# Mixture of experts and attention: one expert's transposes amid another's downs, weight halves with own signals, rotation ahead of values

## The chip, the cores and the metric

One Trainium2 chip, one of its cores. Time is device microseconds of one execution of the whole program; the times below are those of three runs.

## The reference

Two transformer blocks on 256 tokens of width 1024, two layers each, in float32. The second block's last layer is the one the change touches. It attends with 16 heads of 64 (8 with a forget gate, 8 with rotary positions), projects, and then runs a mixture of eight experts:

```python
def moe_swiglu(t, router, w_gate, w_up, w_down):
    logits = (t @ router).astype(jnp.float32)
    top_logits, top_idx = lax.top_k(logits, TOP_K)
    gates = jax.nn.softmax(top_logits, axis=-1)
    combine = jnp.sum(jax.nn.one_hot(top_idx, N_EXPERTS, dtype=jnp.float32) * gates[..., None], axis=1)
    out = jnp.zeros_like(t)
    for e in range(N_EXPERTS):
        out = out + combine[:, e:e + 1].astype(t.dtype) * swiglu(t, w_gate[e], w_up[e], w_down[e])
    return out
```

Each expert has gate and up weights of 1024 x 3584 and down weights of 3584 x 1024; each token goes to two of the eight.

## The kernel before

Everything is written out by hand: five engines, each with its own list of instructions, and semaphores between them. `Steps` names the signals of one engine in the order in which it gives them, so a step's place in that list has to follow the order of the instructions.

**Attention** (`pairs_tensor`, L3686) takes heads in eight pairs, the first four without rotary (fox), the last four with it (moba). For pair p PE does the scores (L3651), the next pair's queries and keys (L3597), the transposes of pair p's weights (L3666), the next pair's values (L3623), the next pair's rotation (L3634; a drain where there is no rotary) and pair p's outputs (L3681). ACT copies queries and keys (L3715), transposed weights (L3742) and values (L3720); DVE does the rope from the rotation (L3757 to L3760), on which the next scores wait.

**Experts.** The router ranks the experts by their load; rank r of the four fullest and rank r of the four emptiest make a pair, so there are four pairs, and each pair's hidden width is taken in seven turns of 512: 28 turns. The fuller expert has 128 token places, the emptier 64. In a turn (`duo_step_tensor`, L4243) PE does, in this order:

- the fuller expert's ups for slots 0 and 1 of 256 columns (`many_ups_tensor`, L4167), each as sums of differences (a Strassen scheme of 2 x 2 blocks) for which DVE first subtracts weight blocks (`many_weights_vector`, four subtractions L4506, L4507, L4509, L4511 per slot);
- the transposes of slot 0's hidden rows (L4182) and the emptier expert's ups of both slots (L4210);
- in some turns a piece for other pairs: the scatter of the last pair's sums back to tokens (L4099 for the fuller expert, L4102 for the emptier; turns 0 and 1), the turned gates (L4061; turn 2) or a gather of tokens for the next pair (L4083; turns 3 to 6). There are 12 gather turns, 6 scatter turns and 4 gates turns; what has none of these is called plain;
- slot 0's downs (L4196), the transposes of slot 1's hidden rows (L4182), the emptier expert's transposes (`few_flip_tensor`, L4223), its downs (L4237), and slot 1's downs (L4196).

ACT copies each transposed block back to SBUF (L4380 for the fuller expert, L4349 for the emptier) before the downs may use it. Silu and product of the emptier expert's hidden rows are two ACT operations (L4342) and two DVE operations (L4492), of 64 rows each.

SP issues all loads, in one queue: per turn twelve of 1 MiB (`moe_sync`): gates and ups of the fuller expert (tiles WF and WO, in halves of the 1024 rows, L4023), the same for the emptier (XT and scratch), and four for the downs (L887). There is one buffer for each, so the fuller expert's gates and ups for the next turn are issued when PE has done this turn's ups of both slots, the emptier's after its ups, and the downs' after the downs:

```python
    for s in range(2):
        for both in range(2):
            sp.wait_ge(*slots[both].pe.at("up1", rnds[both] - 1))
        for h in range(2):
            src = ups[s][:, ds(e, 1), h * 4:h * 4 + 4, turn * 512:(turn + 1) * 512]
```

At the end the last pair's scatter (`last_scatter_tensor`) waits for DVE's copies of both sums (L4480 emptier, L4478 fuller), and DVE adds each tile to the tokens (L4462) and normalises.

Of the kernel before, what the change touches and what calls it, by code (L numbers as in the profile page):

```python
# [18 lines left out]
P = 128  # L19
# [7 lines left out]
ALU = mybir.AluOpType  # L27
# [790 lines left out]
ROUND = 2 * P  # L818
# [2673 lines left out]
def declare_fox(k):  # L3492
# [4 lines left out]
    k.pj_pe = Steps(k, "pj_pe", "qk v rot")  # L3497
# [188 lines left out]
def pairs_tensor(k, pe):  # L3686

    fg_sums_tensor(k, pe)
    pair_values_tensor(k, pe, 0)
    pair_rotate_tensor(k, pe, 0)  # L3690
    pe.wait_ge(*k.fg_act.at("rows"))
    pe.wait_ge(*k.fg_pool.at("sel"))
    for p in range(ATTN_PAIRS):
# [8 lines left out]
        if more:  # L3702
            pair_values_tensor(k, pe, p + 1)
            pair_rotate_tensor(k, pe, p + 1)
        else:
            out_part_tensor(k, 3, 0, 0, OLDER[5:6])
# [99 lines left out]
def declare_moe(k):  # L3806
# [14 lines left out]
    k.flips_pe = Steps(k, "flips_pe", "t0 t1 flip")  # L3821
    k.flips_act = Steps(k, "flips_act", "t0 t1 flip")
# [191 lines left out]
def wide_gates_sync(k, sp, e, kind, n):  # L4014
# [3 lines left out]
    for s in range(2):  # L4018
        for both in range(2):
            sp.wait_ge(*slots[both].pe.at("up1", rnds[both] - 1))  # L4020
        for h in range(2):
            src = ups[s][:, ds(e, 1), h * 4:h * 4 + 4, turn * 512:(turn + 1) * 512]
            sp.dma_start(slots[s].wide[:, h * 4:h * 4 + 4, :], src.rearrange("p e kb n -> p (e kb) n")  # L4023
                         ).then_inc(slots[s].gu_in, 16)
# [67 lines left out]
def duo_scatter_tensor(k, pe, pair, tile, bank):  # L4092

    if tile == 0:
        for kind in (FEWER, MANY):
            pe.wait_ge(*k.sums_dve.at(f"y{kind}", pair))
    cols = slice(tile * P, (tile + 1) * P)
    for half in range(2):
        k.nc.tensor.matmul(k.PS[:, bank + half, :], k.gatedt[:, MANY, cols], k.ye[:, MANY, half * 512:(half + 1) * 512],  # L4099
                           start=True, stop=False)  # L4100
    for half in range(2):
        mm = k.nc.tensor.matmul(k.PS[:, bank + half, :], k.gatedt[ROWS[half], FEWER, cols],  # L4102
                                k.ye[ROWS[half], FEWER, 0:512], start=False, stop=True)
    mm.then_inc(*k.sums_pe.done(f"sc{tile}"))
# [81 lines left out]
def many_down_tensor(k, pe, n, s):  # L4186
# [7 lines left out]
    for f in range(2):  # L4194
# [22 lines left out]
def few_flip_tensor(k, pe, n):  # L4217

    slots, rnds = turn_slots(k, FEWER, n)
    for s in range(2):  # L4220
        pe.wait_ge(*slots[s].dve.at("h1", rnds[s]))
# [21 lines left out]
def duo_step_tensor(k, pe, pair, turn):  # L4243
# [14 lines left out]
    many_down_tensor(k, pe, n, 0)  # L4258
    many_turn_tensor(k, pe, n, 1)
    few_flip_tensor(k, pe, n)  # L4260
# [76 lines left out]
def few_silu_scalar(k, act, n):  # L4337
# [661 lines left out]
```

## Time and profile before

| | |
|---|---|
| three runs: median (lowest to highest) | 3082.94 us (3079.12 to 3086.73) |
| the profiled execution: time, span | 3083.38 us, 3081.6 us |
| busy in the span: PE, PE weight loads, DVE, ACT | 2966.4, 2027.5, 1604.7, 614.0 us |
| chain that ended last, by engine | PE 86%, DVE 4%, DMA 3%, issue 2%, ACT 1%, DVE's sequencer 1% |
| slices 29 to 40 of 40 (the experts): PE busy, DMA busy | 9 tenths, 9 tenths (the last: 6 both) |
| granted TensorE clock, mean | 0.986 |

Busy times are shares of one execution on its one core. PE's matmuls are pipelined: a row's duration holds the way through the array too, so that the next start, not the end, tells how long PE was taken. Stretches are given in us from the start of the span; the experts' turns begin at 2139.95.

### The profile page before, as it was taken

To read this page: it belongs to the slowest core of one execution; us is meant where nothing else is said; L and a number is where in the kernel's file an instruction comes from. 1 tells how busy PE (TensorE), PEld (TensorE's weight loads), DVE (VectorE), ACT (ScalarE), POOL (GpSimd) and SP (SyncE) were. 2 spreads that over 40 slices of the span, in tenths; PEclk is the share of its full clock that TensorE was granted. 3 is DMA by queue.
4 is the path that set the end of the run, shared out by engine and by line. 5 is a ranking of instruction groups with operands and counts; after the bars stand their busy time and mean duration, and the time that the engine had idled before them with its cause. 6 is when DMAs were issued, how large, how long until landed. Compare 5 with 4: busy or idle time off the path is not lost.

```text
span 3081.6 us, 45358 instructions
## 1 busy us (share of the span) xinstructions
PE 2966.4 (96%) x18391; PEld 2027.5 (66%) x18391; DVE 1604.7 (52%) x3044; ACT 614.0 (20%) x1500; POOL 108.8 (4%) x122
## 2 busy tenths in 40 slices
PE   7999998999999999999998999997999999999998
PEld 3566666588696677695786795875555555555554
DVE  2567766456476433476365375233454454454444
ACT  2332332010010123200212100221222222222212
POOL 1111112000000000000000000000000000000000
PEclk8999999999999999999999999998999999999999
DMA  7333116456355422364310365325999999999996
GB/s 254 122 109 135 51 56 262 162 191 204 123 184 186 150 71 73 94 208 163 105 59 15 117 213 164 117 62 180 390 391 383 369 386 382 368 388 382 370 389 238
DMA packets 361234, 636.90 MB, mean 207 GB/s; under 512 B 11950, under 2 KB 190741, under 8 KB 353725
## 3 DMA queue, kind: packets, MB, share of 16 engines
q1 hardware_dynamic: 355677, 612.49, 56.1%
q0 software_dynamic: 5344, 21.46, 2.1%
q8 instruction: 148, 2.42, 0.3%
q14 instruction: 65, 0.53, 0.0%
HBM read 632.70 MB, written 1.20 MB: 206 GB/s over the span
## 4 chain that ended last, share of the span: by engine, by line
PE 86%; DVE 4%; DMA 3%; issue 2%; ACT 1%; DVEq 1%; PEld 1%; SPq 0%; PEldq 0%; ACTq 0%
PE PS L1092 13%; PE PS L4167 11%; PE PS L1112 7%; PE PS L1651 7%; PE PS L4196 5%; PE PS L4210 5%; PE PS L1045 4%; PE PS L4237 2%; PE PS L707 2%; PE PS L2226 2%; PE PS L3597 2%; PE PS L1126 2%; PE PS L2222 2%; PE PS L1796 1%; PE PS L1811 1%
## 5 line engine op out<-in xcount | busy, mean ns | idle before, releaser
L1651 PE MATMUL PS<-XT,WH 128*128 128x512 f32 x512 | 241.4, 597 | 1.8 <-ACT XT L484 1.8
L4167 PE MATMUL PS<-WF,scratch 128*64 128x256 f32 x896 | 204.3, 381 | 0.0
L4167 PEld LDWEIGHTS PS<-WF,scratch 128*64 128x64 f32 x896 | 122.1, 138 | 57.2 <-issue 1.3
L4167 PE MATMUL PS<-WO,scratch 128*64 128x256 f32 x672 | 154.2, 379 | 0.0
L4534 DVE TENSOR_TENSOR WH<-WH,PS 128x256 f32<-128x256 f32 x56 | 23.5, 420 | 231.2 <-ACT WH L4366 231.2
L1651 PEld LDWEIGHTS PS<-XT,WH 128*128 128x128 f32 x512 | 89.2, 192 | 69.1 <-issue 66.6
L1092 PE MATMUL PS<-scratch 128*128 128x128 f32 x896 | 118.3, 275 | 0.0
L4237 PE MATMUL PS<-OT,WH 128*64 128x512 f32 x448 | 102.3, 598 | 14.8 <-ACT WH L4349 14.8
L1092 PEld LDWEIGHTS PS<-scratch 128*128 128x128 f32 x896 | 109.1, 192 | 0.0
L4506 DVE TENSOR_TENSOR scratch<-WO,WF 128x1024 f32<-128x1024 f32 x28 | 34.3, 1225 | 138.8 <-issue 98.1
L4167 PE MATMUL PS<-WO,rope 128*64 128x256 f32 x448 | 105.8, 379 | 0.0
L4196 PE MATMUL PS<-WO,scratch 128*128 128x512 f32 x224 | 103.6, 605 | 0.0
L4210 PE MATMUL PS<-XT,WO 128*64 128x256 f32 x896 | 102.9, 382 | 0.0
L4196 PE MATMUL PS<-WF,scratch 128*128 128x512 f32 x224 | 102.0, 598 | 0.0
L4210 PE MATMUL PS<-scratch,WO 128*64 128x256 f32 x896 | 101.4, 379 | 0.0
L1045 PE MATMUL PS<-XT,WO 128*128 128x256 f32 x448 | 97.8, 379 | 0.0
L1045 PEld LDWEIGHTS PS<-XT,WO 128*128 128x128 f32 x448 | 84.9, 190 | 13.1 <-issue 1.9
L4167 PE MATMUL PS<-scratch,rope 128*64 128x128 f32 (+1 forms) x672 | 81.5, 319 | 12.0 <-DVE rope L4524 8.8
L4167 PEld LDWEIGHTS PS<-WO,scratch 128*64 128x64 f32 x672 | 92.1, 137 | 0.0
L1189 ACT ACTIVATE scratch<-scratch 128x512 f32<-128x512 f32 x32 | 20.2, 630 | 348.7 <-DVEq L1257 348.7
L4210 PEld LDWEIGHTS PS<-scratch,WO 128*64 128x64 f32 x896 | 64.2, 137 | 32.5
L4210 PEld LDWEIGHTS PS<-XT,WO 128*64 128x64 f32 x896 | 61.7, 137 | 33.2 <-issue 4.7
(668 smaller groups left out, 6092.5 us busy)
## 6 DMA issues: line engine op xcount, KB each, us to landing
WF<-in_moe_wg SPq DMA_DIRECT2D x56, 1024.0 KB, 7.2
WO<-in_moe_wu SPq DMA_DIRECT2D x56, 1024.0 KB, 11.4
XT<-in_moe_wg SPq DMA_DIRECT2D x56, 1024.0 KB, 11.3
scratch<-in_moe_wu SPq DMA_DIRECT2D x56, 1024.0 KB, 14.2
OT<-in_moe_wd SPq DMA_DIRECT2D x56, 1024.0 KB, 14.4
WO<-in_ada_w SPq DMA_DIRECT2D x36, 1024.0 KB, 7.0
WF<-in_moe_wd SPq DMA_DIRECT2D x28, 1024.0 KB, 14.2
WO<-in_moe_wd SPq DMA_DIRECT2D x28, 1024.0 KB, 15.1
```

The costliest lines, as they stand in the source:

```text
L707: mm = k.nc.tensor.matmul(k.PS[:, tile * 2 + half, :], k.OT[:, kb, tile * P:(tile + 1) * P], k.WO[:, kb, half * 512:(half + 1) * 512], sta ...
L1045: mm = k.nc.tensor.matmul(k.PS[:, bank, w * L:(w + 1) * L], slot.gu[:, w, kb, f * P:(f + 1) * P], k.XT[:, kb, col:col + L], start=kb == 0, ...
L1092: mm = k.nc.tensor.matmul(k.PS[:, 4 + 2 * w + bank, at * P:(at + 1) * P], weights(i), tokens(i), start=i == 0, stop=i == KB // 2 - 1)
L1112: mm = k.nc.tensor.matmul(k.PS[:, bank, :], tokens, weights, start=p == 0, stop=last)
L1126: mm = k.nc.tensor.matmul(k.PS[:, 2 * tile + half, :], k.hidden[p][:, f, tile * P:(tile + 1) * P], dn[:, f, half * 512:(half + 1) * 512], ...
L1651: mm = k.nc.tensor.matmul(k.PS[:, n % 2, :], k.gdn_w[n][:, kb, :], k.XT[:, kb, :], start=kb == 0, stop=kb == KB - 1)
L2222: mm = nc.tensor.matmul(ps[:, 1, :], w[:, kb, :], k.XT[:, kb, :], start=kb == 0, stop=kb == KB - 1)
L2226: mm = nc.tensor.matmul(ps[:, 2, tile * P:(tile + 1) * P], k.XT[:, kb, tile * P:(tile + 1) * P], w[:, kb, :], start=kb == 0, stop=kb == KB ...
L4167: mm = nc.tensor.matmul(k.PS[rows, at, c], tokens[:, kb, :], weights[:, kb, n:n + width], start=kb == 0, stop=kb == K2 - 1)
L4196: mm = k.nc.tensor.matmul(k.PS[:, half, :], k.hidm[:, f, :], slot.dn[:, f, half * 512:(half + 1) * 512], start=(turn, s, f) == (0, 0, 0), ...
L4210: mm = k.nc.tensor.matmul(k.PS[ROWS[s], 3, w * ROUND:(w + 1) * ROUND], k.xtf[n // E_TURNS % 2][:, kb, :], slots[w].wide[:, kb, s * ROUND:( ...
L4237: mm = k.nc.tensor.matmul(k.PS[ROWS[half], 2, :], k.few_ht[:, f, s * FEW:(s + 1) * FEW], slots[s].dn[:, f, half * 512:(half + 1) * 512], s ...
```

## The change

Seven edits, in attention and experts:

1. Attention: in each pair the rotation (or the drain in its place) comes before the values.
2. Experts, PE: the emptier expert's transposes stand between the two halves (f = 0, 1) of slot 0's downs, slot 1's transposes after both; ACT copies in the same order.
3. The emptier expert's silu and product are one operation each of 128 rows.
4. SP: the fuller expert's gates and ups are loaded by halves, first half of both and then second half of both; the first halves signal one semaphore and the second halves the other.
5. DVE: the first subtraction waits for the first halves alone, the second for the rest.
6. Scatter: the emptier expert's products come first and open the sum, the fuller expert's close it.
7. The last scatter does the emptier expert's products for both tiles before the fuller expert's.

On PE, in a pair with rotary, from the transposes to the scores: before

```order
L3666 MATMUL PS<-mats,scratch 128x128 [waits at_dve]
L3666 MATMUL PS<-mats,scratch 128x128 x2
L3623 MATMUL PS<-scratch,XT 128x128 [waits pj_act,dma_pair_w21]
L3623 MATMUL PS<-scratch,XT 128x128 x15
L3634 MATMUL PS<-scratch,mats 128x512 [waits pj_act]
L3681 MATMUL PS<-scratch 64x128 [waits at_act,pj_act]
```

and now

```order
L3666 MATMUL PS<-mats,scratch 128x128 [waits at_dve]
L3666 MATMUL PS<-mats,scratch 128x128 x2
L3634 MATMUL PS<-scratch,mats 128x512 [waits pj_act]
L3623 MATMUL PS<-scratch,XT 128x128 [waits pj_act,dma_pair_w21]
L3623 MATMUL PS<-scratch,XT 128x128 x15
L3681 MATMUL PS<-scratch 64x128 [waits at_act,pj_act]
```

The rotation (L3634), which waits for ACT's copy of queries and keys, moved ahead of the sixteen matmuls of the values.

On PE, in a plain turn of the experts, from the emptier expert's ups to its downs: before

```order
L4210 MATMUL PS<-scratch,WO 64x256 x15
L4196 MATMUL PS<-WF,scratch 128x512 [waits flips_act,ffna_down_weights]
L4196 MATMUL PS<-WF,scratch 128x512 x3
L4182 MATMUL PS<-mats,WH 128x128 [waits ffnb_dve]
L4182 MATMUL PS<-mats,WH 128x128
L4223 MATMUL PS<-mats,WH 128x128 [waits fourth_dve,third_dve]
L4223 MATMUL PS<-mats,WH 128x128
L4237 MATMUL PS<-OT,WH 64x512 [waits third_down_weights,flips_act]
```

and now (lines from here on are two higher, or one after the transposes)

```order
L4212 MATMUL PS<-scratch,WO 64x256 x15
L4198 MATMUL PS<-WF,scratch 128x512 [waits flips_act,ffna_down_weights]
L4198 MATMUL PS<-WF,scratch 128x512
L4224 MATMUL PS<-mats,WH 128x128 [waits third_dve]
L4224 MATMUL PS<-mats,WH 128x128
L4198 MATMUL PS<-WF,scratch 128x512 [waits flips_act,ffna_down_weights]
L4198 MATMUL PS<-WF,scratch 128x512
L4184 MATMUL PS<-mats,WH 128x128 [waits ffnb_dve]
L4184 MATMUL PS<-mats,WH 128x128
L4238 MATMUL PS<-OT,WH 64x512 [waits third_down_weights,flips_act]
```

The emptier expert's transposes (L4223, now L4224) moved from behind slot 1's transposes into the middle of slot 0's four downs.

On DVE, the four subtractions of one slot, before and now (`ffna_up_weights` and `ffnb_up_weights` are the two load semaphores):

```order
L4506 TENSOR_TENSOR scratch<-WO,WF 128x1024 [waits ffna_pe,ffnb_up_weights,ffna_up_weights]
L4507 TENSOR_TENSOR WO<-WO 128x4x256
L4509 TENSOR_TENSOR scratch<-WO,scratch 128x1024
L4511 TENSOR_TENSOR scratch<-WF,scratch 128x1024
```

```order
L4504 TENSOR_TENSOR scratch<-WO,WF 128x1024 [waits ffna_pe,ffna_up_weights]
L4506 TENSOR_TENSOR WO<-WO 128x4x256 [waits ffnb_up_weights]
L4508 TENSOR_TENSOR scratch<-WO,scratch 128x1024
L4510 TENSOR_TENSOR scratch<-WF,scratch 128x1024
```

The second wait moved from the first subtraction to the second. The diff, cut to its core:

```diff
-    k.pj_pe = Steps(k, "pj_pe", "qk v rot")
+    k.pj_pe = Steps(k, "pj_pe", "qk rot v")
...
 def pairs_tensor(k, pe):
...
+    pair_rotate_tensor(k, pe, 0)
     pair_values_tensor(k, pe, 0)
-    pair_rotate_tensor(k, pe, 0)
...
+            pair_rotate_tensor(k, pe, p + 1)
             pair_values_tensor(k, pe, p + 1)
-            pair_rotate_tensor(k, pe, p + 1)
...
-    k.flips_pe = Steps(k, "flips_pe", "t0 t1 flip")
-    k.flips_act = Steps(k, "flips_act", "t0 t1 flip")
+    k.flips_pe = Steps(k, "flips_pe", "t0 flip t1")
+    k.flips_act = Steps(k, "flips_act", "t0 flip t1")
...
 def wide_gates_sync(k, sp, e, kind, n):
...
-    for s in range(2):
-        for both in range(2):
-            sp.wait_ge(*slots[both].pe.at("up1", rnds[both] - 1))
-        for h in range(2):
+    for slot, rnd in zip(slots, rnds):
+        sp.wait_ge(*slot.pe.at("up1", rnd - 1))
+    for a in range(2):
+        for b in range(2):
+            h, s = (a, b) if kind == MANY else (b, a)
             src = ups[s][:, ds(e, 1), h * 4:h * 4 + 4, turn * 512:(turn + 1) * 512]
             sp.dma_start(slots[s].wide[:, h * 4:h * 4 + 4, :], src.rearrange("p e kb n -> p (e kb) n")
-                         ).then_inc(slots[s].gu_in, 16)
+                         ).then_inc(slots[h if kind == MANY else s].gu_in, 16)
...
-def duo_scatter_tensor(k, pe, pair, tile, bank):
+def duo_scatter_tensor(k, pe, pair, tile, bank, kinds=(FEWER, MANY)):
...
+    cols = slice(tile * P, (tile + 1) * P)
+    for kind in kinds:
+        if tile == 0:
             pe.wait_ge(*k.sums_dve.at(f"y{kind}", pair))
...
+            mm = k.nc.tensor.matmul(k.PS[:, bank + half, :], gates, sums, start=kind == FEWER, stop=kind == MANY)
+    if MANY in kinds:
+        mm.then_inc(*k.sums_pe.done(f"sc{tile}"))
...
 def few_flip_tensor(k, pe, n):
...
-    for s in range(2):
-        pe.wait_ge(*slots[s].dve.at("h1", rnds[s]))
+    pe.wait_ge(*slots[0].dve.at("h1", rnds[0]))
...
 def duo_step_tensor(k, pe, pair, turn):
...
-    many_down_tensor(k, pe, n, 0)
+    many_down_tensor(k, pe, n, 0, (0,))
+    few_flip_tensor(k, pe, n)
+    many_down_tensor(k, pe, n, 0, (1,))
     many_turn_tensor(k, pe, n, 1)
-    few_flip_tensor(k, pe, n)
     few_down_tensor(k, pe, n)
...
 def last_scatter_tensor(k, pe):
...
-    for tile in range(2):
-        duo_scatter_tensor(k, pe, EXPERT_PAIRS - 1, tile, (6, 4)[tile])
+    for kind in (FEWER, MANY):
+        for tile in range(2):
+            duo_scatter_tensor(k, pe, EXPERT_PAIRS - 1, tile, (6, 4)[tile], (kind,))
...
 def few_silu_scalar(k, act, n):
...
-    for s in range(2):
-        act.activation(k.few_sg[ROWS[s], :], k.PS[ROWS[s], 3, 0:ROUND], ACT.Silu
-                       ).then_inc(*slots[s].act.both("silu0", "silu1"))
+    act.activation(k.few_sg, k.PS[:, 3, 0:ROUND], ACT.Silu).then_inc(*slots[0].act.both("silu0", "silu1"))
...
+    few_flip_scalar(k, act, n)
     many_hidden_scalar(k, act, n, 1)
-    few_flip_scalar(k, act, n)
...
 def many_weights_vector(k, dve, n, s):
...
-    for slot, rnd in zip(slots, rnds):
-        dve.wait_ge(slot.gu_in, (rnd + 1) * 32)
+    dve.wait_ge(slots[0].gu_in, (rnds[0] + 1) * 32)
     if n:
         dve.wait_ge(*slots[s].pe.at("up1", rnds[s] - 1))
     tt(row[0], w[0][1], w[0][0], ALU.subtract)
+    dve.wait_ge(slots[1].gu_in, (rnds[1] + 1) * 32)
     tt(w[0][1], w[1][1], w[0][1], ALU.subtract)
```

## Rows read from the trace of the kernel before

**Rows 1.** One turn each, by windows: gather, scatter, gates, plain; columns: us, busy us per engine, PE clock, DMA share, GB/s.

```profile
2484.16:2517.03 32.87, 32.34 (x240) 18.99 (x238) 15.26 (x22) 7.51 (x23) 0.00 (x0) 1.00 1.03 386
2382.59:2417.14 34.55, 34.02 (x240) 18.63 (x238) 16.49 (x23) 6.96 (x21) 0.00 (x0) 1.00 1.00 375
2219.09:2251.13 32.04, 31.50 (x236) 18.06 (x234) 17.34 (x32) 7.61 (x23) 0.00 (x0) 1.00 1.04 393
2981.80:3014.32 32.52, 31.11 (x232) 17.70 (x230) 15.27 (x22) 6.95 (x21) 0.00 (x0) 1.00 1.04 389
```

**Rows 2.** Waits, experts: waiting engine and line, then releaser: us in total, times, longest us.

```profile
PEld PS L4167 <- DVE scratch L4511: 15.2, 15, 1.7
PE PS L4237 <- ACT WH L4349: 14.8, 28, 0.5
...
PE PS L4167 <- DVE scratch L4511: 3.1, 6, 0.9
```

**Rows 3.** Timeline, plain turn, end of emptier ups to its downs: start us, us, engine, line.

```profile
2956.50 3.70 PE L4196 MATMUL PS<-WF,scratch 128*128 128x512 f32 x8
...
2957.19 0.87 DVE L4492 TENSOR_TENSOR WH<-WH,PS 64x256 f32<-64x256 f32 x2 [2.29 <-ACT WH L4342]
...
2960.04 0.38 PE L4182 MATMUL PS<-mats,WH 128*128 128x128 f32 x2
...
2960.26 0.38 PE L4223 MATMUL PS<-mats,WH 128*128 128x128 f32 x2
...
2960.74 0.38 ACT L4349 ACTIVATE WH<-PS 128x256 f32<-128x256 f32 x1
...
2961.17 2.37 PE L4237 MATMUL PS<-OT,WH 128*64 128x512 f32 x10 [0.53 <-ACT WH L4349]
```

**Rows 4.** Timeline, loads of the last plain turn on SP, DVE and PE.

```profile
2981.80 0.93 SPq L4023 DMA_DIRECT2D WF<-in_moe_wg  x2
...
2996.75 1.22 DVE L4506 TENSOR_TENSOR scratch<-WO,WF 128x1024 f32<-128x1024 f32 x1 [6.27 <-issue]
...
3001.77 1.09 PE L4167 MATMUL PS<-scratch,rope 128*64 128x128 f32 x16 [0.88 <-DVE scratch L4511]
```

**Rows 5.** Timeline, DVE, first subtractions of the first turn.

```profile
2133.18 1.22 DVE L4506 TENSOR_TENSOR scratch<-WO,WF 128x1024 f32<-128x1024 f32 x1 [9.97 <-DMA WO<-in_moe_wu]
2134.32 1.22 DVE L4507 TENSOR_TENSOR WO<-WO 128x1024 f32<-128x1024 f32 x1
```

**Rows 6.** Timeline, one pair with rotary: copy, values, rotation, outputs, scores.

```profile
2033.36 0.60 ACT L3715 ACTIVATE scratch<-PS 128x512 f32<-128x512 f32 x1 [3.21 <-PE PS L3597]
...
2033.82 3.74 PE L3623 MATMUL PS<-scratch,XT 128*128 128x128 f32 x32
...
2037.39 1.02 PE L3634 MATMUL PS<-scratch,mats 128*128 128x512 f32 x2
...
2038.35 0.88 PE L3681 MATMUL PS<-scratch 128*64 128x128 f32 x12
...
2040.57 0.93 PE L3651 MATMUL PS<-scratch 64*128 64x128 f32 x8 [1.34 <-DVE scratch L3760]
```

**Rows 7.** Timeline, PE, gates transposes before downs.

```profile
2924.54 0.66 PE L4061 MATMUL PS<-mats,scratch 128*128 128x128 f32 x4
...
2925.04 3.60 PE L4196 MATMUL PS<-WF,scratch 128*128 128x512 f32 x8
```

**Rows 8.** Timeline, PE, two transposes before the emptier ups.

```profile
2516.74 0.44 PE L4182 MATMUL PS<-mats,WH 128*128 128x128 f32 x2
2517.11 3.67 PE L4210 MATMUL PS<-XT,WO 128*64 128x256 f32 x32
```

**Rows 9.** Timeline, tail: copy of the sum, scatter, adds.

```profile
3065.31 1.23 DVE L4478 COPY scratch<-PS 128x1024 f32<-128x1024 f32 x1 [2.93 <-PE PS L4196]
...
3068.56 1.13 PE L4102 MATMUL PS<-scratch 64*128 64x512 f32 x4
...
3072.71 1.22 DVE L4462 TENSOR_TENSOR X<-X,PS 128x1024 f32<-128x1024 f32 x1 [0.43 <-PE PS L4102]
```

More of the change, by code:

```diff
@@ L4089, in duo_gates_tensor @@
     gates_turned(k, kind, 4 + kind).then_inc(*k.duo_pe.done(f"tr{kind}"))
-def duo_scatter_tensor(k, pe, pair, tile, bank):
-    if tile == 0:
-        for kind in (FEWER, MANY):
+def duo_scatter_tensor(k, pe, pair, tile, bank, kinds=(FEWER, MANY)):
+    cols = slice(tile * P, (tile + 1) * P)
+    for kind in kinds:
+        if tile == 0:
             pe.wait_ge(*k.sums_dve.at(f"y{kind}", pair))
[L4097 to L4104, printed above, removed]
+        for half in range(2):
+            if kind == FEWER:
+                gates, sums = k.gatedt[ROWS[half], FEWER, cols], k.ye[ROWS[half], FEWER, 0:512]
+            else:
+                gates, sums = k.gatedt[:, MANY, cols], k.ye[:, MANY, half * 512:(half + 1) * 512]
+            mm = k.nc.tensor.matmul(k.PS[:, bank + half, :], gates, sums, start=kind == FEWER, stop=kind == MANY)
+    if MANY in kinds:
+        mm.then_inc(*k.sums_pe.done(f"sc{tile}"))
 def gather_tensor(k, pe, e):
@@ L4183, in many_turn_tensor, with many_down_tensor @@
     mm.then_inc(*k.flips_pe.done(f"t{s}"))
-def many_down_tensor(k, pe, n, s):
+def many_down_tensor(k, pe, n, s, fs=range(2)):
     slots, rnds = turn_slots(k, MANY, n)
@@ L4193, in many_down_tensor @@
         pe.wait_ge(*k.sums_dve.at("y0", pair - 1))
-    for f in range(2):
+    for f in fs:
         for half in range(2):
@@ L4488, in few_vector @@
         dve.wait_ge(*k.flips_pe.at("flip", n - 1))
-    dve.wait_ge(*slots[1].pe.at("up1", rnds[1]))
-    for s in range(2):
-        dve.wait_ge(*slots[s].act.at("silu1", rnds[s]))
-        k.nc.vector.tensor_tensor(k.few_h[ROWS[s], :], k.few_sg[ROWS[s], :], k.PS[ROWS[s], 3, ROUND:2 * ROUND],
-                                  ALU.mult).then_inc(*slots[s].dve.both("h0", "h1"))
+    dve.wait_ge(*slots[0].act.at("silu1", rnds[0]))
+    k.nc.vector.tensor_tensor(k.few_h, k.few_sg, k.PS[:, 3, ROUND:2 * ROUND], ALU.mult
+                              ).then_inc(*slots[0].dve.both("h0", "h1"))
 def many_weights_vector(k, dve, n, s):
```

## The prediction

> **What bounds the kernel now.** I read the page first: its chain of work is 86% PE, and the last 12 of its 40 slices, the experts, have PE at 9 tenths and the DMA engines at 9 tenths together. So a saving there has to be paid by two resources, and the chain alone doesn't say which is next. Four stretches of one turn each settle the order [rows 1]. In a turn that also gathers for the next pair PE is busy 32.34 of 32.87 us, in one that also scatters 34.02 of 34.55; the rest is the same 0.53 us. In a gates turn of the first pair and in a plain turn of the last pair the turn lasts 32.04 and 32.52 us while PE is busy only 31.50 and 31.11 us: something else holds it. Those two rows also show the transfers at 393 and 389 GB/s, the gather turn 386 and the scatter turn 375. A turn loads 12 MiB, 12.58 MB; at 393 GB/s that is **32.0 us**. So the long turns are bound by PE with 0.9 to 2.5 us of transfer time to spare, and the short ones by the loads.
>
> The waits say what the 0.53 us is: 28 times, once a turn, the emptier expert's downs stand until ACT L4349 has copied the transposed hidden rows, 14.8 us in total; and the first ups wait for DVE's last subtraction, L4511: 15 of their weight loads 15.2 us in total, of which 3.1 us in 6 turns leave PE idle [rows 2]. In a plain turn [rows 3] PE starts the first slot's downs at 2956.50, transposes slot 1 at 2960.04 and the emptier expert's rows at 2960.26, and its next downs start at 2961.17, after the copy at 2960.74. Those hidden rows were ready at 2957.19 + 0.87 = 2958.06, two us earlier.
>
> The wait for DVE is a loop [rows 4]: the four loads of the fuller expert's gates and ups are issued at 2981.80, as the last turn's ups end; DVE starts at 2996.75, when they have landed (14.95 us); PE starts at 3001.77, released by the fourth subtraction, 5.0 us later. Subtractions start 1.14 us apart where nothing is between them [rows 5].
>
> Attention has its own small wait: in the four pairs with rotary, PE's scores stand 1.34 us for DVE L3760, because the rotation came after the values [rows 6].
>
> **The change part by part.** Sums are made against the profiled execution, 3083.38 us, which is 0.44 above the median shown, 3082.94.
>
> *Attention.* Values (3.57 us from 2033.82 to 2037.39) and rotation change places [rows 6]. The rope then runs beside the values, and scores follow the outputs directly. The wait goes, with some 0.07 us of matmul overlap: 1.41. New: the rotation needs ACT's copy of queries and keys, which ends at 2033.36 + 0.60 = 2033.96, while PE is free at 2033.82; with 0.06 us for the signal PE stands 0.2 us. Net 1.2, four times: **4.7 us**. Bounds: 5.6 without the new wait, 3.6 if it is 0.5 each. In the four pairs without rotary the rotation is only a drain that moves; one drain stands in each place, so nothing. Load waits on the values' signal move by under 1 us, and the next pair's weights are loaded a pair ahead.
>
> *Transposes amid the downs.* Nothing is added: two transposes move up by half the downs, and their copy by ACT runs beside the other half (1.7 us against 0.38). The switches have neighbours in the trace. From four transposes to the same downs takes 0.50 us, 0.06 more than four at 0.11 [rows 7]; from two transposes to 64-column matmuls takes 0.37, 0.15 more than two at 0.11 [rows 8]. Downs to the emptier expert's downs is now 2961.17 - 2956.50 = 4.67 us [rows 3]. Then: 3.54 for the downs, 0.22 for the emptier expert's transposes, 0 to 0.06 to return, 0.22 + 0.15 for slot 1: 4.13. I take 0.54 a turn; bounds 0.35 (both switches at the dearer price and the return at 0.2) and 0.69 (PE's idle time and its lost overlap). Are the hidden rows there? With one ACT and one DVE operation in place of two each they end before 2958.06; the transposes come at 2956.50 + 1.82 = 2958.3. This lies on the path in 12 gather turns, 6 scatter turns and the last turn: 19 x 0.54 = **10.3 us** (6.7 to 13.1). The gather turn becomes 32.3 us, still over the transfers' 32.0.
>
> *Halves with own signals.* SP issues the same four loads in another order, one gate half, one up half, twice; waits and bytes are the same. The first halves of both land 2 MiB before the last, some 5 us at the present rate, so DVE's first subtraction runs in its idle time and three remain behind the last landing: 1.14 us less [rows 5]. At the first turn PE waits for this chain, so 1.14 comes off: **1.1 us** (0 to 1.2). What DVE has queued ahead (the emptier expert's product, the token sums) ends well before the landing, and nothing new waits behind the first subtraction.
>
> *Turns that waited for the loads.* Nine: the first three, the gates turn of the other three pairs, three plain turns of the last pair. Each could give 0.54 plus its wait (3.1 us, with 0.07 of overlap lost at each 3.7): in all 9 x 0.54 + 3.7 = 8.6 us; if the transfers give nothing, 0. The three gates turns follow scatter turns, in which the queue ran dry, and the subtractions come 1.14 us earlier: I take them in full, 3 x 0.54 and a fifth of the 3.7, 2.3 us. For the other six the 32.0 us binds; they gain the 1.14 once per run of three and the small gaps of the queue, 3.7 us together. **6.0 us.**
>
> *Scatter.* Within the turns it keeps its matmuls and switches: 0. In the last scatter the emptier expert's matmuls (1.13 us a tile at most) run from 3065.3 on, while DVE copies the fuller expert's sum and PE stood anyway [rows 9]; they end at 3067.3, and the fuller expert's first tile, 1.9 us from that copy's end at 3066.54 to 3068.56 now, ends at 3069.2. DVE's first add, now behind 3068.56 + 1.13, follows there, and the last tile's add, behind it and one product of its length (1.2 us each), at 3071.6 in place of 3072.71: **1.1 us** (0.5 to 1.3).
>
> Sum: 4.7 + 10.3 + 1.1 + 6.0 + 1.1 = 23.2. 3083.4 - 23.2 = 3060.2; against the median **3060 us**. All low ends give 10.8 off (3072), all high ends 29.8 (3053).
>
> A rule that speaks against all this: the Trainium skill, "DMA: Bandwidth & Descriptors", section Specifications, puts HBM at about 358 GB/s per core. By it a turn could not be under 12.58 MB / 358 GB/s = 35.1 us, and no change on PE would show there; the trace disagrees, with 393 GB/s in a turn of 32.04 us [rows 1].
>
> **The rivals.**
>
> *The loads bind sooner.* For: the queue's gap after each issue (the wait until data flows again) may not close when PE comes sooner. Against: gather turns move only 386 of 393 GB/s. If the floor is 32.6 us, gather turns give 0.27 each (3.2), the nine turns 1.5, scatter turns 6 x 0.54 = 3.2, and the rest stays at 6.9: 14.8 off, **3068**. Its extreme is that the transfers bind every turn already, so that only attention, start and end are left, 6.9 off, 3076; since the turns' rates differ from 375 to 393 GB/s [rows 1], I give that 0.01. The page's 358 GB/s above would mean this case.
>
> *The gap stays on PE.* The two more switches between transposes and downs give back 0.4 of the 0.54. Against: 0.06 [rows 7]. Then 19 x 0.15 + 4 + 6.9 = 13.8 off, **3069**.
>
> *Slower.* Loads that change between the gates' and the ups' tensor every MiB move slower. To be slower by 0.3% they must lose 9.2 us and the 6.9 gained elsewhere, 16 us over 27 turns, so turns of 33.7 in the mean, where the 24 between 2219.09 and 3014.32 now have 33.1 [rows 1]. With 32.0 of transfers that takes 1.7 us more in the four loads, which last 10.9 us at 386: it decides at about **335 GB/s**. At 320 GB/s, 2.2 us more, turns are 34.2 and the time is 3083 + 27 x 1.1 - 7 = **3106**. Against: the present turn changes tensor five times in twelve loads and still holds 393.
>
> *It doesn't do what it says.* If the emptier expert's rows are late, the wait moves in front of its transposes, in the middle of the downs: 0.2 us of margin in plain turns by the old end of 2958.06, over 1.4 in gather turns, where the gathering stands between. Then the long turns gain all the same, the plain ones less: about the first rival's 3068.
>
> **How the numbers follow.** Forecast 0.66, loads sooner 0.14, loads binding every turn 0.01, gap on PE 0.11, late rows 0.03, slower 0.03, more than the sum's upper end 0.02. The range that holds 8 in 10 takes the forecast's own bounds and both milder rivals: 3053 to 3071. A measurement of this kernel tells 0.3%, 9.2 us, from no change (its three runs lie 7.6 us apart). Under 3073.7 is faster: all of the forecast and most of the two milder rivals, 0.90. Both milder rivals at once, or loads that bind every turn, end within 0.3%: 0.07. Slower: 0.03.
>
> **What would show it.** Right: the emptier expert's wait for the copy gone from 28 to 0; gather turns 32.3 us and scatter turns 34.0; DVE's first subtraction apart from the other three, which start at the landing; the scores' wait for L3760 gone, with about 0.2 us before the rotation. Wrong: gather turns at 32.6 or more with PE waiting for DVE's sums (first rival), or with a gap between transposes and downs (second); four loads that take over 16 us from issue to DVE's second subtraction with the queue full (third).

## The result and the profile after

| | before | changed |
|---|---|---|
| three runs: median (lowest to highest) | 3082.94 us (3079.12 to 3086.73) | 3055.3 us (3053.34 to 3059.3) |
| ratio of the two, 95% interval | | 0.9901 [0.9875, 0.9927] |
| the profiled execution: time, span | 3083.38, 3081.6 us | 3053.34, 3051.2 us |
| granted TensorE clock, mean | 0.986 | 0.988 |

The change is 27.6 us faster by the medians; 3060 was forecast, with a range from 3053 to 3071. Medians, here and below, are of fast runs: one run of e3 lasted 5929.94 us, at a mean granted clock of 0.904, and is left out.

By the page of the changed kernel PE has 86% of the chain that ended last, as before, and DMA went from 3% to 5%. One turn each by windows, in the order gather, scatter, gates of the first pair, gates of a later pair, plain (columns as in [rows 1]):

```profile
2466.30:2498.57 32.27, 32.27 (x239) 18.91 (x239) 14.94 (x21) 7.24 (x22) 0.00 (x0) 1.00 1.04 393
2367.45:2401.19 33.74, 33.74 (x239) 18.71 (x239) 16.07 (x22) 6.68 (x20) 0.00 (x0) 1.00 1.04 392
2206.20:2238.09 31.89, 31.44 (x235) 18.05 (x235) 16.84 (x31) 7.27 (x22) 0.00 (x0) 1.00 1.04 394
2434.94:2466.30 31.36, 31.36 (x235) 18.02 (x235) 16.84 (x31) 7.25 (x22) 0.00 (x0) 1.00 1.01 375
2953.40:2985.48 32.08, 31.05 (x231) 17.66 (x231) 14.94 (x21) 6.69 (x20) 0.00 (x0) 1.00 1.04 394
```

The gather turn lasts 32.27 us where it lasted 32.87, the scatter turn 33.74 for 34.55 [rows 1], and in both PE is busy without a gap. A gates turn behind a scatter turn is now also PE alone, 31.36. The first pair's gates turn and the plain turn still hold 0.45 and 1.03 us in which PE isn't busy, at 394 GB/s: these wait for loads.

One of the twelve gather turns, the third of the first pair, also waits a little: 32.55 us here, 32.50 and 32.46 in two more executions of the changed kernel (e0 and e10 below). The very first turn, 32.73 to 33.78 us, is another case: in e10 it lasts 33.76 us with PE busy for all of them, at a granted clock of 0.92. The gather turn that waits, by windows:

```profile
2290.21:2322.76 32.55, 32.34 (x239) 18.95 (x238) 14.21 (x22) 7.23 (x22) 0.00 (x0) 1.00 1.04 393
```

The waits of the experts (window 2160 to 3050; us in total, times, longest us). No row is left in which PE's downs (now L4238) wait for ACT; it was 14.8 us in 28 turns [rows 2]. What is left of PE's waiting is the last subtraction (now L4510), and the first subtractions of each slot (L4504, then L4506) now wait for loads one after the other:

```profile
DVE WO L4506 <- DMA WO<-in_moe_wu: 90.3, 26, 4.4
...
DVE scratch L4504 <- DMA WO<-in_moe_wu: 20.2, 14, 2.4
...
PE PS L4169 <- DVE scratch L4510: 3.6, 6, 1.0
...
PEld PS L4224 <- DVE WH L4491: 1.2, 5, 0.2
```

The plain turn by its timeline, issue of the loads to the next turn's ups:

```profile
2953.54 0.37 SPq L4024 DMA_DIRECT2D WF<-in_moe_wg  x1
...
2960.67 1.98 PE L4198 MATMUL PS<-WF,scratch 128*128 128x512 f32 x4
...
2962.49 0.38 PE L4224 MATMUL PS<-mats,WH 128*128 128x128 f32 x2
2962.71 1.88 PE L4198 MATMUL PS<-WF,scratch 128*128 128x512 f32 x4
2962.91 0.38 ACT L4350 ACTIVATE WH<-PS 128x256 f32<-128x256 f32 x1 [1.68 <-PE PS L4224]
2963.80 1.23 DVE L4504 TENSOR_TENSOR scratch<-WO,WF 128x1024 f32<-128x1024 f32 x1 [2.01 <-DMA WO<-in_moe_wu]
2964.43 0.38 PE L4184 MATMUL PS<-mats,WH 128*128 128x128 f32 x2
2964.74 3.65 PE L4238 MATMUL PS<-OT,WH 128*64 128x512 f32 x16
...
2969.18 1.22 DVE L4506 TENSOR_TENSOR WO<-WO 128x1024 f32<-128x1024 f32 x1 [4.16 <-DMA WO<-in_moe_wu]
...
2973.06 0.77 PE L4169 MATMUL PS<-scratch,rope 128*64 128x128 f32 x10 [1.03 <-DVE scratch L4510]
```

Downs to the emptier expert's downs is 2964.74 - 2960.67 = 4.07 us; it was 4.67 [rows 3]. The copy L4350 starts at 2962.91 and has 1.45 us to spare. The first subtraction starts 5.38 us before the second, in DVE's idle time, and from the second to the ups it is 3.88 us, where it was 5.02 from the first [rows 4].

### The profile page after: what moved, and what is told of

Its sections match the earlier page's. It is cut to its first block, busy times and chain, and to the rows that moved or that the text cites. A ratio compares the mean times of both kernels' runs of the same rounds, so it can differ in the third digit from the quotient of the medians.

```text
span 3051.2 us, 45189 instructions
## 1 busy us (share of the span) xinstructions
PE 2958.9 (97%) x18391; PEld 2022.1 (66%) x18391; DVE 1591.2 (52%) x3016; ACT 606.3 (20%) x1472; POOL 109.7 (4%) x122
## 4 chain that ended last, share of the span: by engine, by line
PE 86%; DMA 5%; DVE 4%; issue 1%; ACT 1%; DVEq 1%; PEld 1%; SPq 0%; PEldq 0%; ACTq 0%
PE PS L1092 13%; PE PS L4169 11%; PE PS L1112 7%; PE PS L1651 7%; PE PS L4198 5%; PE PS L4212 5%; PE PS L1045 5%; DMA WO<-in_moe_wu 4%; PE PS L4238 2%; PE PS L707 2%; PE PS L2226 2%; PE PS L3597 2%; PE PS L1126 2%; PE PS L2222 2%; PE PS L1796 1%
## 5 line engine op out<-in xcount | busy, mean ns | idle before, releaser
L4506 DVE TENSOR_TENSOR WO<-WO 128x1024 f32<-128x1024 f32 x56 | 68.4, 1222 | 99.7 <-DMA WO<-in_moe_wu 99.7
L4238 PE MATMUL PS<-OT,WH 128*64 128x512 f32 x448 | 102.3, 598 | 0.0
## 6 DMA issues: line engine op xcount, KB each, us to landing
XT<-in_moe_wg SPq DMA_DIRECT2D x56, 1024.0 KB, 11.3
```

The costliest lines, as they stand in the source:

```text
L4238: mm = k.nc.tensor.matmul(k.PS[ROWS[half], 2, :], k.few_ht[:, f, s * FEW:(s + 1) * FEW], slots[s].dn[:, f, half * 512:(half + 1) * 512], s ...
L4506: tt(w[0][1], w[1][1], w[0][1], ALU.subtract)
```

## Where the time came from, by stages

The same stages in all executions. "First score" is the start of the first pair's scores, "steps" the time from there to the eighth pair's, "chain" from the first issue of the experts' loads to the first ups, "gather", "scatter" and "nine" the sums of those 12, 6 and 9 turns (start of ups to start of ups), "tail" from the last turn's ups to the end of the span, "rest" from the first score to the end. Each is a difference of two starts in a timeline; us.

| run | timed median | first score | steps | chain | gather | scatter | nine | tail | rest |
|---|---|---|---|---|---|---|---|---|---|
| before | 3082.94 | 1967.22 | 103.88 | 20.51 | 394.40 | 207.24 | 292.03 | 47.96 | 1114.4 |
| changed | 3055.3 | 1961.96 | 99.69 | 19.24 | 387.51 | 202.47 | 285.82 | 46.22 | 1089.2 |
| e0 (changed) | 3062.73 | 1973.48 | 99.69 | 19.36 | 387.45 | 202.47 | 287.10 | 46.21 | 1088.8 |
| e1 | 3063.16 | 1970.83 | 103.87 | 19.35 | 387.28 | 202.47 | 286.13 | 46.23 | 1093.0 |
| e2 | 3074.02 | 1964.12 | 99.69 | 19.10 | 394.40 | 206.06 | 288.93 | 46.82 | 1101.5 |
| e3 | 3068.39 | 1970.48 | 99.69 | 20.24 | 389.82 | 202.47 | 293.12 | 46.20 | 1098.1 |
| e4 | 3061.17 | 1965.11 | 99.69 | 19.12 | 387.24 | 203.65 | 287.17 | 47.34 | 1090.7 |
| e5 | 3055.29 | 1976.01 | 99.69 | 19.20 | 387.23 | 202.47 | 283.55 | 46.21 | 1084.9 |
| e6 | 3058.79 | 1968.07 | 98.04 | 19.05 | 387.55 | 202.47 | 285.96 | 46.22 | 1087.1 |
| e7 | 3069.86 | 1964.97 | 99.69 | 20.42 | 387.75 | 202.47 | 291.78 | 46.24 | 1094.9 |
| e8 (before) | 3088.76, one run | 1972.79 | 103.94 | 20.24 | 394.49 | 207.24 | 292.18 | 47.96 | 1114.2 |
| e9 (as e6) | 3059.18 | 1970.36 | 98.04 | 19.02 | 387.41 | 202.47 | 286.64 | 46.21 | 1087.8 |
| e10 (changed) | 3058.17 | 1964.13 | 99.69 | 19.35 | 387.43 | 202.47 | 286.97 | 46.22 | 1088.7 |

Stages bound by PE repeat to 0.1 us. What varies is the code ahead of attention, the same in all kernels but for the place of one drain: its end lies between 1961.96 and 1976.01. Most of the spread arises at 1600 to 1680 us, where the granted clock averages 0.81 in e0 (first score 1973.48) and 0.98 in the first execution of the changed kernel (1961.96). So the spans of the two executions shown, 30.4 us apart, hold 5.3 us that the change did not make. From the first score on, two executions of before take 1114.4 and 1114.2 us, three of the changed kernel 1089.2, 1088.8 and 1088.7: the difference is **25.4 us**, in steps 4.2, chain 0.9 to 1.3, gather 6.9, scatter 4.8, nine 4.9 to 6.4, tail 1.7; what is left is the routing ahead of the chain, 48.1 and 48.3 us in before, 48.3, 46.5 and 46.5 in the changed kernel. That last part goes with the granted clock and not with the change (e6 below), so the stages that the change touches add up to 23.4 to 25.3 us.

## The experiments

Each is an edit of the changed kernel and is read against it. Ratios are to runs of before beside them: 3085.26 us for e0 to e3, 3084.46 for e4 to e7, 3087.55 for e8 to e10.

**e0, the changed kernel again**, five rounds, no edit.

> The changed kernel again. Theory: of the 30.2 us between the two profiled executions, some 5 us lie before the attention, in code that both kernels share, and belong to the TensorE clock of that execution and not to the change; what belongs to the change is 24 to 25 us: experts' first ups come 5.7 us earlier than before when both are counted from the first scores of attention, the 27 turns from there to the last turn's ups take 875 to 877 us, and the tail 46.2. So the median stands 23 to 28 us under the kernel before, and the stretch before attention differs between executions by microseconds. Rival: the 5 us before attention are an effect of the change; then that stretch is shorter here too, by about 5 us, and in every other kernel that keeps the change.

Median 3062.73 us, ratio 0.9926 [0.991, 0.9941]: 22.5 us faster beside these runs, just under the 23 to 28 expected. The stages are those of the first execution, but attention begins 11.5 us later, so the expectation's rival falls.

**e1, values ahead of the rotation again.**

```diff
-    k.pj_pe = Steps(k, "pj_pe", "qk rot v")
+    k.pj_pe = Steps(k, "pj_pe", "qk v rot")
...
+            pair_values_tensor(k, pe, p + 1)
             pair_rotate_tensor(k, pe, p + 1)
-            pair_values_tensor(k, pe, p + 1)
```

> Attention alone undone: the values before the rotation. Theory: each of the four pairs with rotary lasts 1.1 us longer, with the scores' wait of 1.34 us for DVE's rope back and PE's stand of 0.3 us before the rotation gone: 4.4 us, about 3060. Nothing changes in the experts. Rival: the rotation ahead was not what moved the attention (the scores would have been held by another wait): under 1 us.

The time, 3063.16 us, ratio 0.9925 [0.9909, 0.9941], can't be told from e0's. The trace can: the steps are 103.87 us again, 4.18 more. One pair with rotary, scores to scores, by the timeline, first of e1:

```profile
2028.90 0.93 PE L3651 MATMUL PS<-scratch 64*128 64x128 f32 x8 [1.34 <-DVE scratch L3760]
...
2036.77 0.82 PE L3666 MATMUL PS<-mats,scratch 128*128 128x128 f32 x6
2037.42 3.74 PE L3623 MATMUL PS<-scratch,XT 128*128 128x128 f32 x32
2040.99 1.02 PE L3634 MATMUL PS<-scratch,mats 128*128 128x512 f32 x2
...
2044.16 0.93 PE L3651 MATMUL PS<-scratch 64*128 64x128 f32 x8 [1.34 <-DVE scratch L3760]
```

and of the changed kernel:

```profile
2019.21 0.93 PE L3651 MATMUL PS<-scratch 64*128 64x128 f32 x8
...
2027.07 0.82 PE L3666 MATMUL PS<-mats,scratch 128*128 128x128 f32 x6
2027.92 1.12 PE L3634 MATMUL PS<-scratch,mats 128*128 128x512 f32 x2
2028.89 3.73 PE L3623 MATMUL PS<-scratch,XT 128*128 128x128 f32 x32
2032.55 0.88 PE L3681 MATMUL PS<-scratch 128*64 128x128 f32 x12
2033.36 0.93 PE L3651 MATMUL PS<-scratch 64*128 64x128 f32 x8
```

A step of 15.26 us became 14.15. The scores' wait is gone. In its place the rotation starts 0.85 us after the transposes, where in e1 the values start 0.65 after them: PE stands 0.2 us for the copy of queries and keys, as forecast, and the outputs start 3.66 us after the values, 0.09 more than the rotation did in e1. The pairs without rotary step by 14.14 to 14.15 in the changed kernel, in place of 13.98 to 14.09 in e1: the drain costs more in its new place.

**e2, the emptier expert's transposes behind slot 1's again**, with ACT's copies.

```diff
-    many_down_tensor(k, pe, n, 0, (0,))
+    many_down_tensor(k, pe, n, 0)
+    many_turn_tensor(k, pe, n, 1)
     few_flip_tensor(k, pe, n)
-    many_down_tensor(k, pe, n, 0, (1,))
-    many_turn_tensor(k, pe, n, 1)
...
+    many_hidden_scalar(k, act, n, 1)
     few_flip_scalar(k, act, n)
-    many_hidden_scalar(k, act, n, 1)
```

> The emptier expert's transposes behind slot 1's transposes again, everything else as changed. Theory: the wait for ACT's copy is back 28 times, gather turns 32.87 us in place of 32.27, scatter turns 34.3 in place of 33.75, gates turns 31.96 in place of 31.36; the turns bound by the loads (first three, last plain ones) keep their 31.9 to 32.1: 22 x 0.60 = 13 us more, about 3068. Rival, the loads bind the long turns too: the long turns change by less than 0.3 us each, under 7 us in all.

3074.02 us, ratio 0.9962 [0.9949, 0.9975], 11.3 us over e0; from the first score on it is 12.7, for 13 expected. Its wait, and a gather turn by windows:

```profile
PE PS L4238 <- ACT WH L4349: 14.3, 27, 0.5
```

```profile
2471.95:2504.81 32.86, 32.33 (x239) 18.97 (x239) 14.94 (x21) 7.14 (x22) 0.00 (x0) 1.00 1.04 391
```

The wait is back with its 0.53 us a turn and the gather turns sum to 394.40, before's to the hundredth. So in a turn bound by PE the place of the transposes alone decides 0.60 us: the idle 0.53 and 0.07 of overlap lost at it. The scatter turns do not come back whole: 34.34 us each, not 34.54 (e4 shows why). Edit 3, one silu and one product in place of two each, stays in e2; with the gather turns at before's sum, it is worth nothing there by itself.

**e3, loads in the old order, first subtraction behind all of them.** **e7, the new order and the two signals kept, first subtraction behind both.**

```diff
-            h, s = (a, b) if kind == MANY else (b, a)
+            h, s = b, a
...
-                         ).then_inc(slots[h if kind == MANY else s].gu_in, 16)
+                         ).then_inc(slots[s].gu_in, 16)
...
-    dve.wait_ge(slots[0].gu_in, (rnds[0] + 1) * 32)
+    for slot, rnd in zip(slots, rnds):
+        dve.wait_ge(slot.gu_in, (rnd + 1) * 32)
...
-    dve.wait_ge(slots[1].gu_in, (rnds[1] + 1) * 32)
```

e7 has the last two pieces of this diff only (the waits).

> Loads in the old order and DVE's first subtraction behind all of them, everything else as changed. Theory: all four subtractions follow the last landing, so the chain from issue to the first ups is 1.14 us longer; gather turns had 0.15 to 1.5 us of slack, so most of them now wait for DVE and take 32.4 to 32.9 us; gates turns 31.9 to 32.4 in place of 31.36; first turn 1.1 later; scatter turns (slack 2.1 to 3.9) unchanged: 8 to 11 us more, about 3064. Rival: the loads' bytes per turn bind whatever the signals; then only the first turn's 1.1 us come back and the other turns keep their times within 0.2.

> Loads by halves in the new order with their two signals, but DVE's first subtraction waits for both signals; everything else as changed. Theory: what the halves give comes from the first subtraction's place ahead of the last landing, so this is the run with one signal again: first turn 1.1 us later, gates turns 31.9 to 32.3, 27 turns in 883 to 887 us. Rival: the new order of the transfers itself is faster; then 27 turns in 876 to 878 us.

3068.39 us, ratio 0.9946 [0.9925, 0.9967], and 3069.86 us, ratio 0.9951 [0.9935, 0.9967]. In both the chain is about 1 us longer again (20.24 and 20.42 for 19.24 to 19.36) and the nine turns give back 4.7 to 7.3 us. The turn shown above, in e7 by its timeline:

```profile
2976.59 1.22 DVE L4505 TENSOR_TENSOR scratch<-WO,WF 128x1024 f32<-128x1024 f32 x1 [6.54 <-DMA WO<-in_moe_wu]
...
2981.60 1.09 PE L4169 MATMUL PS<-scratch,rope 128*64 128x128 f32 x16 [1.32 <-DVE scratch L4510]
```

From the landing to the ups it is 5.01 us again, against 3.88. That the wait alone brings this back, with the loads in the new order, shows the cause: one subtraction less behind the last landing. The order is what makes that possible. What the order does by itself is not settled: from the first score on e3 takes 3.2 us more than e7, 2.1 of it in gather turns, in one execution each. The 27 turns of e7 sum to 882.0 us, 1 us under the range expected. That most gather turns would wait in e3 was wrong: three of the twelve do, by 0.3 to 1.4 us, the others stay at 32.27 to 32.33. In e7 four do, by 0.1 to 0.2 us. Why just these turns wait stays open.

**e4, scatter in the old order**, in the turns and at the end.

```diff
-def duo_scatter_tensor(k, pe, pair, tile, bank, kinds=(FEWER, MANY)):
+def duo_scatter_tensor(k, pe, pair, tile, bank, kinds=(MANY, FEWER)):
...
-    for kind in (FEWER, MANY):
-        for tile in range(2):
-            duo_scatter_tensor(k, pe, EXPERT_PAIRS - 1, tile, (6, 4)[tile], (kind,))
+    for tile in range(2):
+        duo_scatter_tensor(k, pe, EXPERT_PAIRS - 1, tile, (6, 4)[tile])
```

> Scatter in the old order, fuller expert first, also at the end; everything else as changed. Theory: the six scatter turns take 33.94 us in place of 33.75 (the switch of tile shapes costs 0.19 more between the emptier expert's products and the downs), and the tail from the last turn's ups is 47.4 in place of 46.2: 2.3 us in all. Rival: the order costs nothing within the turns (as the prediction had it) and only the tail's 1.1 us come back.

3061.17 us, ratio 0.9928 [0.9899, 0.9956]; by time no difference, by trace the tail is 1.12 us longer and each scatter turn 0.20:

```profile
2403.63:2437.57 33.94, 33.94 (x239) 18.60 (x239) 16.08 (x22) 6.68 (x20) 0.00 (x0) 1.00 1.01 379
```

The time from e4's scatter to the transposes in the downs, then the same in the changed kernel:

```profile
2410.89 3.04 PE L4104 MATMUL PS<-scratch 128*128 128x512 f32 x8
2413.87 1.98 PE L4198 MATMUL PS<-WF,scratch 128*128 128x512 f32 x4
2415.69 0.38 PE L4224 MATMUL PS<-mats,WH 128*128 128x128 f32 x2
```

```profile
2374.72 3.04 PE L4104 MATMUL PS<-scratch 64*128 64x512 f32 x8
2377.59 1.88 PE L4198 MATMUL PS<-WF,scratch 128*128 128x512 f32 x4
2379.31 0.38 PE L4224 MATMUL PS<-mats,WH 128*128 128x128 f32 x2
```

PE is busy throughout in both orders and has the same matmuls. From the scatter's start to the downs it takes 2.98 us in e4 and 2.87 in the changed kernel, and from there to the transposes 1.82 and 1.72: together this is the whole 0.20. In the old order the products with weights of 64 rows, the emptier expert's, stand between the fuller expert's scatter and the downs, which both have weights of 128 by 128. In the new order they stand ahead of both, so the fuller expert's scatter and the downs are neighbours, and PE changes the shape of its weights once less on the way.

The tail of the changed kernel, for [rows 9]:

```profile
3035.93 5.62 PE L4104 MATMUL PS<-scratch 64*128 64x512 f32 x16
3036.04 1.23 DVE L4479 COPY scratch<-PS 128x1024 f32<-128x1024 f32 x1 [2.93 <-PE PS L4198]
3039.87 1.22 DVE L4463 TENSOR_TENSOR X<-X,PS 128x1024 f32<-128x1024 f32 x1 [2.61 <-PE PS L4104]
...
3042.32 1.21 DVE L4463 TENSOR_TENSOR X<-X,PS 128x1024 f32<-128x1024 f32 x1
```

The scatter runs on from the downs without a stand, and the last add follows the first with one product between them.

**e5, lighter loads**: for the emptier expert's downs one block of two is loaded, so that they use old data for the other.

```diff
-        expert_downs_sync(k, sp, e, n, slots[s], rnds[s], s)
+        at = 4 * (n % E_TURNS) + 2 * s
+        sp.wait_ge(*slots[s].pe.at("down1", rnds[s] - 1))
+        sp.dma_start(slots[s].dn[:, 0:1, :], expert_weights(k)[1][:, ds(e, 1), at:at + 1, :].rearrange("p e b n -> p (e b) n")
+                     ).then_inc(slots[s].dn_in, 16)
```

> The emptier expert's downs load one block of two in each slot, 11 MiB a turn in place of 12, so those downs use old data for the other block; everything else as changed. Theory: the turns that still wait (the second and third 31.9 us, the last three plain ones 31.3 to 32.1) are bound by bytes; with 29.4 us of transfers they fall to PE's own 30.96 (31.36 with the gates), and no turn waits for DVE's subtractions: 27 turns in 871 to 873 us in place of 876. Gather, scatter and gates turns stay at 32.27, 33.75 and 31.36. Rival, the chain from issue to subtractions binds and not the bytes: those turns keep 31.9.

3055.29 us, ratio 0.9899 [0.9873, 0.9926]. A plain turn by windows:

```profile
2964.96:2996.12 31.16, 31.04 (x231) 17.65 (x231) 14.86 (x21) 6.68 (x20) 0.00 (x0) 1.00 1.00 373
```

Scatter and later gates turns are unchanged, and so are the gather turns but for the one that waited, which falls to 32.27. The nine turns get shorter, 283.55 us for 285.82 to 287.10, and all but the first come to PE's own 30.97 to 31.36. The first, 33.86, has PE busy throughout, at a granted clock of 0.91. So it is bytes that bound the others, for 2.3 to 3.6 us in all; with fewer of them no other limit shows.

**e6 and e9, rotation between the two token tiles of the values.**

```diff
     for tile in range(2):
+        if tile:
+            pair_rotate_tensor(k, pe, p)
         for kb in range(KB):
...
-            pair_rotate_tensor(k, pe, p + 1)
             pair_values_tensor(k, pe, p + 1)
```

> Rotation between the values of the two token tiles, everything else as changed. Theory: PE's stand of 0.3 us before the rotation, waiting for ACT's copy of queries and keys, is filled by the first tile's values, and the rope still ends before the scores: each pair with rotary 13.85 us in place of 14.15, 1.2 us in all. Pairs without rotary drain in the middle of the values: their 14.15 may change by 0.2 either way. Rival: the rope is now late for the scores, which wait again: over 14.15.

> The version with the rotation between the two token tiles of the values, beside the changed kernel (next run) on one chip. Theory: 1.7 us less than the changed kernel in the steps between pairs, and the same turns; 0.05%, which the two medians can show only if their spread is under that, so the medians lie within 4 us of each other, in either order. Rival (what comes free in attention is taken back by later waits for loads): the steps are 98.0 us again but the stretch from the last score to the experts' first ups grows by as much.

> The changed kernel once more, as the neighbour of the two runs ahead of it. Theory: steps between pairs 99.7 us, gather turns 32.27, scatter turns 33.75, 27 turns 875.8 to 877.1, tail 46.2; time between 3055 and 3063 us, ratio 0.99 to 0.993. Rival (the first comparison's 0.9901 and the second's 0.9926 are different behaviours of the experts): 27 turns outside that range.

3058.79 us, ratio 0.9916 [0.9895, 0.9938], and beside the changed kernel 3059.18, 0.9912 [0.9896, 0.9927], against 3058.17, 0.9914 [0.99, 0.9927]. One pair of e6:

```profile
2024.55 0.93 PE L3653 MATMUL PS<-scratch 64*128 64x128 f32 x8
...
2033.07 1.95 PE L3625 MATMUL PS<-scratch,XT 128*128 128x128 f32 x16
2034.86 1.02 PE L3636 MATMUL PS<-scratch,mats 128*128 128x512 f32 x2
2035.72 1.95 PE L3625 MATMUL PS<-scratch,XT 128*128 128x128 f32 x16
...
2038.40 0.93 PE L3653 MATMUL PS<-scratch 64*128 64x128 f32 x8
```

The step is 13.85: half of the values covers the copy, the other half the rope, and PE waits for neither. The steps sum to 98.04, 1.65 us under the changed kernel's, in both runs. From the first score on these runs take 1087.1 and 1087.8 us, 0.9 to 2.1 less; the time can't show it. The routing ahead of the experts' loads was longer in both (last score to first issue 47.86 and 48.00 us, for 46.52, 46.53 and 48.26 in the changed kernel), as the expectation's rival has it, but it goes with the granted clock. That stretch by windows, first e10, then e6:

```profile
2063.82:2110.34 46.52, 40.62 (x166) 23.39 (x164) 15.49 (x59) 10.67 (x30) 2.52 (x4) 0.94 0.10 25
```

```profile
2066.11:2113.97 47.86, 41.90 (x166) 24.84 (x164) 15.49 (x59) 10.78 (x30) 2.52 (x4) 0.91 0.09 25
```

The length follows the mean clock, 0.94 and 0.91 here: e0 has 0.94 in 46.53 us and e9 0.91 in 48.00. It does so with one kernel too, as the first execution of the changed kernel has 0.88 in 48.26. Nor is the gain lost by it: the first turn, in which the clock is still low for a while, is 1.2 to 1.4 us shorter in e6 and e9 than in e0 and e10 (32.38 and 32.53 us for 33.78 and 33.76).

**e8, the kernel before again.**

> The kernel before, once more, for its stages. Theory (5.1 us of the difference between the two profiled executions lie ahead of attention, in code that both share, and come from stretches at half the granted clock, not from the change): the first score of attention starts somewhere between 1962 and 1976 us, as in the eight executions of changed kernels, and more than 1 us away from the 1967.2 of the execution shown is as likely as not; the sum of the seven steps between the scores of pairs repeats at 103.9 us within 0.1, the gather turns at 32.87, the scatter turns at 34.54, the 27 turns at 893.7 within 1.5. Rival (the stretch ahead of attention is longer in the kernel before for a reason of its own): the first score at 1967.2 within 0.5 again.

Its first score is at 1972.79 us, so the rival (1967.2 again) falls; steps, gather, scatter and tail repeat to 0.1 us. What differs ahead of attention is the granted clock, as these windows of the first execution of before show (columns as in [rows 1]). Below them is a group of matmuls that lies in them (L3610) and the one ahead of it, in before, then the same in the changed kernel:

```profile
1953.00:1957.00 4.00, 4.00 (x25) 4.00 (x25) 0.35 (x2) 0.34 (x2) 0.00 (x0) 0.64 0.83 330
1957.00:1961.00 4.00, 4.00 (x21) 4.00 (x20) 0.18 (x1) 0.22 (x1) 0.00 (x0) 0.51 0.00 0
```

```profile
1951.65 4.57 PE L3532 MATMUL PS<-WH,XT 128*128 128x8 f32 x32
1956.07 6.15 PE L3610 MATMUL PS<-XT,scratch 128*128 128x128 f32 x32
```

```profile
1949.81 3.64 PE L3532 MATMUL PS<-WH,XT 128*128 128x8 f32 x32
1953.30 3.82 PE L3610 MATMUL PS<-XT,scratch 128*128 128x128 f32 x32
```

In before the clock is at its lower level, 0.5 of full speed (1.2 of 2.4 GHz), for most of these 8 us, with PE busy without a gap in the window in which it falls and in the next. The two groups last 10.57 us from the first start to the last end in before and 7.31 in the changed kernel, at full clock. That is 3.3 us of the 5.3.

## Why the prediction was right and where it was off

The direction, the mechanism of the parts and the order of their sizes held. What failed is the size, in two steps: the term for the transposes was too small, 10.3 us where 12.3 were measured, with the scatter within the turns put at nothing; and the base of the sum, the time of code that the change leaves alone, was taken as fixed and is not. By the prediction's own terms, us:

| term | predicted | measured | shown by |
|---|---|---|---|
| attention | 4.7 | 4.2 | e1 |
| transposes, 12 gather and 6 scatter turns, last turn | 10.3 | 12.3 (6.9 + 4.8 + 0.6) | e2, and e4 for 1.2 of it |
| first turn's chain | 1.1 | 0.9 to 1.3 | e3, e7, e8 |
| nine turns that waited for loads | 6.0 | 4.9 to 6.4 | e3, e5, e7 |
| last scatter | 1.1 | 1.1 | e4 |
| sum | 23.2 | 23.4 to 25.3; 25.4 from the first score on, routing with it | e0, e8, e10 |

- **Long turns, mis-sized.** "I take 0.54 a turn" should have been 0.60, as 4.07 for 4.67 in the plain turn and 32.27 for 32.87 in the gather turns show. The return to the downs (taken at 0 to 0.06) costs nothing, and from slot 1's transposes to the emptier expert's downs it takes 0.31, not the 0.22 + 0.15 taken from the neighbour with the emptier ups [rows 8]. And, on the scatter, "Within the turns it keeps its matmuls and switches: 0" was wrong: which matmuls stand next to which did change, and that is 0.20 us in each of six turns (e4).
- **Attention, mis-sized by half a microsecond.** Four times the net of 1.2 is 4.8, not 4.7, and 4.2 was measured. The new stand for ACT's copy was 0.2 us as taken. What was left out is the 0.09 between values and outputs, and "so nothing" for the pairs without rotary: their drain costs up to 0.17 a pair there.
- **Loads.** That 32.0 us of transfers would bind the plain turns and the first pair's second and third held: 31.9 to 32.1 at 394 GB/s, but for the first of the three plain ones (31.3 to 31.7); and e5 takes bytes away and these turns fall to PE's own time. That the three gates turns behind scatter turns would gain in full held too, 31.36 with PE without a gap. For the very first turn it did not hold: PE is busy through all of it in e0, e5 and e10, at a granted clock of 0.91 or 0.92. Of its gain of 1.0 to 2.3 us a part is that clock, which came up at different moments.
- **The base.** "Sums are made against the profiled execution, 3083.38 us" took the unchanged code as fixed. It isn't: by the same sum the changed execution came out at 3053.3, of which 5.3 us lie ahead of attention. The prediction treated half a microsecond between execution and median as the whole of that doubt; one stretch alone moved by 14 us among thirteen executions. The first comparison's medians lie 27.6 us apart, 4.4 more than the sum's 23.2. From the first score on the difference is 25.4, so about half of the excess comes from the terms and the routing's clock and half from code ahead of attention; that part is chance. In the later comparisons the change brought 22.5 and 29.4 us by medians.
- **The rivals.** Loads that bind sooner: eleven of the twelve gather turns hold 32.27 at 393 GB/s, so no, though the load-bound turns' 31.9 is near: the twelfth waits 0.2 to 0.3 us, and in e3 more of them did. The gap stays on PE: no, it is gone. Slower by alternating tensors: 393 to 394 GB/s with the new order in turns of 32 us, and 15.64 us from issue to the second subtraction in the plain turn, under the 16 named, so no. Late rows: five weight loads of the emptier expert's transposes wait for the product, by 0.2 us at most.
- **The Trainium skill's figure.** The Trainium skill, "DMA: Bandwidth & Descriptors", section Specifications, gives about 358 GB/s per core; here turns of 32 us ran at 393 before and at 393 to 394 after.

## What to carry to other kernels

Where an engine stands for a copy of its own result, put independent work between the two; what to look at is the wait and also which kinds of work become neighbours, which here was worth 0.1 to 0.2 us at places without any wait. Where a chain waits for several loads, pair their halves so that part of the work can start on the first ones: it is the work behind the last landing that counts. And read a change of under 1% from stages that repeat: a change of 4.2 us was plain in the trace and could not be seen in the times.

## What the runs showed that was not expected

- Turns bound by PE repeat to 0.01 us on both chips used, in all kernels that have their order (gather 32.27 where no load is late, scatter 33.74 or 33.75), while the stretch ahead of attention moves by up to 14 us, mostly through the granted clock.
- In before the granted clock fell, from its level of 2.4 to that of 1.2 GHz, while the profile shows PE busy without a gap, in matmuls of 128 x 8 (L3532); in the changed kernel's first execution the same matmuls ran and it did not fall. Why stays open.
- The same matmuls in another order, with no idle time of PE in either, differ by 0.20 us in each scatter turn (33.74 and 33.94), by one change of weight shape: a busy share of 100% does not say that an order is the shortest.
